# A decoder block on one Trainium2 core: v between the first two score steps, the last scores ahead of two gate projections, and the next block's k behind them

## What is computed

```python
h = rms_norm(x, ln_g)
proj = einsum('bsd,de->bse', h, w_in)
(u_pool, g_pool, c_a, c_b, g_conv, q, k, v, g_attn) = split_columns(proj)
y_pool = pool_mixer(u_pool, pool_w, pool_scale)
y_conv = conv_module(c_a, c_b, conv_dw, conv_b, conv_ln_g, conv_ln_b, conv_pw)
y_attn = sliding_window_attention(q, k, v, sinks)   # 8 heads, 2 kv heads, window 128, ALiBi, sinks
y = concat([y_pool * silu(g_pool), y_conv * silu(g_conv), y_attn * silu(g_attn)])
out = rms_norm(x + einsum('bse,ed->bsd', y, w_out), final_g)
```

## Time and profile before

| what | value |
|---|---|
| median of 3 runs | 1454.54 us (1451.94 to 1455.07) |
| the profiled execution's own time | 1452.87 us |
| its span in the profile | 1450.7 us, 20622 instructions |
| busy: PE, DVE, ACT, POOL | 94%, 81%, 38%, 35% |
| mean granted clock of PE | 0.986 |
| chain that ended last | PE 66%, DVE 14%, DMA 8%, ACT 5%, POOL 3% |

### The profile page before, as it was taken

The page is one execution under the profiler, slowest core; times in us unless marked ns, Lnnn a source line. Parts: engine busy times, 40 slices in busy tenths (PEclk is TensorE's granted clock), DMA queues, the critical chain, the costliest instruction groups (busy, mean ns, idle before and its releaser), DMA issues.

```text
span 1450.7 us, 20622 instructions
## 1 busy us (share of the span) xinstructions
PE 1363.4 (94%) x7070; PEld 1112.5 (77%) x7070; DVE 1170.9 (81%) x2365; ACT 549.3 (38%) x1421; POOL 504.8 (35%) x640
## 2 busy tenths in 40 slices
PE   6989898989989899876999999999999999999998
PEld 5867676767778687755888888888888888888886
DVE  4877768685868675554989999989899998888886
ACT  5746555555555554330221221121222243333332
POOL 5254545445354534552010010110101255555552
PEclk9999999999999999988999999999999999999999
DMA  9757482939384736657031230330326756545531
GB/s 214 218 125 263 124 284 89 288 110 268 124 254 153 203 146 162 245 130 222 12 131 54 108 131 24 136 130 14 131 88 250 286 193 213 164 158 163 159 126 73
DMA packets 112426, 230.78 MB, mean 159 GB/s; under 512 B 16464, under 2 KB 74192, under 8 KB 104656
## 3 DMA queue, kind: packets, MB, share of 16 engines
q1 hardware_dynamic: 88192, 205.85, 42.5%
q10 hardware_dynamic: 24144, 23.80, 6.8%
HBM read 131.05 MB, written 98.57 MB: 158 GB/s over the span
## 4 chain that ended last, share of the span: by engine, by line
PE 66%; DVE 14%; DMA 8%; ACT 5%; POOL 3%; issue 2%; SPq 1%; POOLq 0%; ACTq 0%; DVEq 0%
PE wide L346 12%; PE wide L347 12%; PE wide L348 12%; DMA xs<-in_x_dram 5%; PE pair L1239 3%; PE pair L1233 3%; PE pair L1234 3%; DVE m_tail L1994 3%; DVE a_rows L1038 2%; ACT a_rows L909 2%; PE wide L1233 2%; PE wide L1234 2%; PE turn L1202 2%; PE wide L1239 2%; PE turn L347 2%
## 5 line engine op out<-in xcount | busy, mean ns | idle before, releaser
L1994 DVE SCALAR_TENSOR_TENSOR m_tail<-m_tail,m_taps 128x512 f32<-128x512 f32 x480 | 338.5, 750 | 4.6
L1233 PE MATMUL pair<-xT,w_hi 128*128 128x512 f32 x384 | 154.5, 402 | 27.0 <-ACT xT L333 23.5
L845 POOL TENSOR_SCALAR a_rows<-a_rows,a_inv 128x128 f32<-128x128 f32 x256 | 108.4, 443 | 204.1 <-DVE a_inv L1058 204.0
L1736 POOL TENSOR_TENSOR operand_sums<-m_y 128x512 f32<-128x512 f32 x75 | 102.2, 1362 | 167.7 <-PE wide L348 116.6
L108 POOL TENSOR_TENSOR pool_carrier<-pool_carrier 128x1 f32<-128x1 f32 x23 | 14.0, 611 | 394.5 <-DVE m_meanvar L2003 394.5
L1234 PE MATMUL pair<-xT,w_lo 128*128 128x512 f32 x384 | 150.8, 393 | 0.0
L1239 PE MATMUL pair<-xT,w_hi 128*128 128x512 f32 x384 | 149.2, 394 | 0.9 <-DVE xT L339 0.7
L346 PE MATMUL wide<-x_first,w_hi 128*128 128x512 f32 x320 | 125.4, 392 | 0.0
L346 PE MATMUL wide<-xT,w_hi 128*128 128x512 f32 x320 | 125.2, 391 | 0.0
L348 PE MATMUL wide<-x_first,w_hi 128*128 128x512 f32 x320 | 124.6, 389 | 0.0
L348 PE MATMUL wide<-xT,w_hi 128*128 128x512 f32 x320 | 124.5, 389 | 0.0
(11 more groups left out here) (262 smaller groups left out, 3233.8 us busy)
## 6 DMA issues: line engine op xcount, KB each, us to landing
xT_scratch<-xT SPq DMA_DIRECT2D x16, 2048.0 KB, 10.3
p_scratch<-a_rows SPq DMA_DIRECT2D x32, 512.0 KB, 2.6
x_first<-xT_scratch SPq DMA_DIRECT2D x16, 1024.0 KB, 8.7
xT<-xT_scratch SPq DMA_DIRECT2D x16, 1024.0 KB, 9.0
combo_scratch<-stage SPq DMA_DIRECT2D x28, 512.0 KB, 5.3
m_y<-y_scratch ACTq DMA_DIRECT2D x14, 1024.0 KB, 6.6
xs<-in_x_dram SPq DMA_DIRECT2D x20, 512.0 KB, 10.7
a_pT<-p_scratch SPq DMA_DIRECT2D x64, 128.0 KB, 4.7
```

The costliest lines, as they stand in the source:

```text
L845: last = nc.gpsimd.tensor_scalar(probs[b][:, h], probs[b][:, h], inv[:, b, h:h + 1], 0.5, ALU.mult, ALU.mult)
L1233: nc.tensor.matmul(out, w.hi(c)[:, kk, cols], st.hi[:, kk, :], start=(kk == 0), stop=False)
L1736: nc.gpsimd.tensor_tensor(operand_sums[:, i, 1], y_block(q, left), y_block(q, right), SIGN[op]).then_inc(operand_sum, 1)
L1994: nc.vector.scalar_tensor_tensor(out=conv[:, i, :], in0=h[:, i, j:j + TB], scalar=taps[:, i, j:j + 1], in1=conv[:, i, :], op0=ALU.mult, op ...
```

## The change

It moves work in five queues and adds or removes none, apart from waits.

- **PE**: k of block n+1 now stands behind g3 of block n, at the end of the body. A block starts with attend(n-1, 0), then q0 to q3, the fold now in q3; then the wait for q_taken and scores 0; then attend(n-1, 1), v, scores 1, g0, scores 2 (with turn_v), g1, scores 3, g2, g3. q0 and q1 wait for one half of the last scores only.
- **ACT**: scales of the next x stand at the end: part 0 ahead of the exponentials of j = 0, parts 1 and 2 behind those of j = 3, part 3 behind the tanh of g2; then split_hi 0 to 3. The squares stand behind q_hi 1, the copy of v between the exponentials of j = 0 and 1.
- **DVE**: the transposes of the next x stand with their scales (`next_x`), all the inverts of a step behind both halves of take_scores, gate_make one step later, split_lo 0 to 3 behind next_x(3). In block 7 the split of CHUNK_GP stands behind the inverts of j = 3.
- **POOL**: mask(n, 0) behind normalise 1 and mask(n, 1) behind normalise 2; masks 2 and 3 of the block before now stand ahead of the root.
- **SP**: the load of the next x stands first in a block, then the load of the probabilities 2, the store of 3, the load of 3.

```diff
--- before.py
+++ after.py
@@ -739,10 +739,10 @@
             else:
+                st.load(sp, n + 1, (0, 1))
+                load_probs(sp, n - 1, 2)
                 store_probs(sp, n - 1, 3)
-                st.load(sp, n + 1, (0, 1))
-                for j in (2, 3):
-                    load_probs(sp, n - 1, j)
+                load_probs(sp, n - 1, 3)
...
@@ -761,14 +761,14 @@
-        store_probs(sp, NB - 2, 3)
         combos.wait_stored(sp)
...
         sp.wait_ge(st.lo_done, KT * NB)
         for c in (CHUNK_CB, CHUNK_CA, CHUNK_GP):
             w.load(sp, c, (0, 1))
-        for j in (2, 3):
-            load_probs(sp, NB - 2, j)
+        load_probs(sp, NB - 2, 2)
+        store_probs(sp, NB - 2, 3)
+        load_probs(sp, NB - 2, 3)
         sp.wait_ge(xT_stored[PIECES - 1], 16)
         load_xT(sp, x_first, x_first_loaded, xT_scratch, 0, (3,))
...
@@ -860,18 +860,14 @@
             else:
-                mask(n - 1, 1)
+                for j in (2, 3):
+                    mask(n - 1, j)
             if n < NB - 1:
                 st.root(pool, n + 1, carrier)
-            if n > 0:
-                for j in (2, 3):
-                    mask(n - 1, j)
             for j in range(SUB):
                 normalise(n, j)
-                if j == 2:
-                    mask(n, 0)
-                    if n == NB - 1:
-                        mask(n, 1)
+                if j in (1, 2):
+                    mask(n, j - 1)
...
@@ -946,63 +942,63 @@
...
-            elif not final:
+            q_hi(n, 1)
+            if not first and not final:
                 st.square(act, n + 1)
-            q_hi(n, 1)
...
             q_hi(n, 2)
-            if not first and not final:
-                st.scale(act, n + 1, 0)
...
                 w.split_hi(act, CHUNK_CB)
-            else:
-                st.scale(act, n + 1, 1)
             q_hi(n, 3)
-            if not first and not final:
-                st.scale(act, n + 1, 2)
-            for s in combos.of_block(n, (3,)):
+            for s in combos.of_block(n, (3, 4)):
...
-            if first:
-                for part in (0, 1):
-                    st.scale(act, 1, part)
-            act.wait_ge(st.squared, SUB + st.HALF * (n if final else n + 1))
-            copy_out(n, slot("v"), vT)
-            for s in combos.of_block(n, (4,)):
-                combos.split_hi(act, s)
-            if not first and not final:
...
+            def take_v():
+                act.wait_ge(st.squared, SUB + st.HALF * (n if final else n + 1))
+                copy_out(n, slot("v"), vT)
+
...
+            if not final:
+                st.scale(act, n + 1, 0)
+            for kv in range(KV):
+                exps(n, 0, kv)
+            take_v()
+            for kv in range(KV):
+                exps(n, 1, kv)
+            gate_tanh(n, 0)
+            exps(n, 2, 0)
+            spread_v()
+            exps(n, 2, 1)
+            gate_tanh(n, 1)
+            if final:
+                w.split_hi(act, CHUNK_GP)
+            for kv in range(KV):
+                exps(n, 3, kv)
+            if not final:
+                for part in (1, 2):
+                    st.scale(act, n + 1, part)
+            gate_tanh(n, 2)
+            if not final:
                 st.scale(act, n + 1, 3)
-            if first:
-                st.scale(act, 1, 2)
-            for j in range(SUB):
-                exps(n, j, 0)
-                if j == SUB - 1 and not final:
-                    for kk in range(st.AHEAD):
-                        st.split_hi(act, n + 1, kk)
-                if final and j == 2:
-                    w.split_hi(act, CHUNK_GP)
...
-                if j:
-                    gate_tanh(n, j)
-                exps(n, j, 1)
-                if j == 0:
-                    gate_tanh(n, j)
-                if first and j == 0:
...
+                for kk in range(st.AHEAD):
+                    st.split_hi(act, n + 1, kk)
+            gate_tanh(n, 3)
...
@@ -1108,69 +1104,67 @@
...
+            make_k_lo(n)
             if not first:
+                output(dve, n - 1, 0)
                 turn_squares_of_probs(SUB * n - 1)
-            make_k_lo(n)
             make_q_lo(n, 0)
             make_combos(n, (0,))
-            if not first:
-                output(dve, n - 1, 0)
-                if not final:
-                    st.square_more(dve, n + 1)
...
-                if t == 1 and not first and not final:
+                if t == 3 and not final:
                     st.mean(dve, n + 1)
                 make_q_lo(n, t)
-                if t == 3 and not first and not final:
-                    st.turn_squares(dve, n + 1, 1)
+                if t == 1 and not first and not final:
+                    st.square_more(dve, n + 1)
...
-                elif t == 2 and not final:
-                    st.turn_squares(dve, n + 1, 0)
-                elif t == 3 and first:
-                    for part in (0, 1):
-                        st.turn_squares(dve, 1, part)
-                elif t == 3 and not final:
-                    st.turn_squares(dve, n + 1, 2)
...
+            def next_x(part):
+                if not final:
+                    st.turn_squares(dve, n + 1, part)
+
+            take_scores(n, 0, 0)
+            take_scores(n, 0, 1)
             if not first:
                 output(dve, n - 1, 1)
-            for j in range(SUB):
+            inverts(0)
+            for j in range(1, SUB):
                 take_scores(n, j, 0)
-                if j in (1, 2):
-                    turn_squares_of_probs(SUB * n + j - 1)
+                turn_squares_of_probs(SUB * n + j - 1)
                 take_scores(n, j, 1)
-                invert(4 * n + j, j % 2, 0)
-                if j == 3:
-                    turn_squares_of_probs(SUB * n + 2)
-                if first and j < 2:
-                    st.turn_squares(dve, 1, 2 + j)
-                elif j == 0 and not first and not final:
-                    st.turn_squares(dve, n + 1, 3)
-                if j == SUB - 1 and not final:
-                    st.split_lo(dve, n + 1, 0)
-                if j:
-                    gate_make(n, j)
-                if j == SUB - 1 and not final:
-                    for kk in range(1, PIECE):
-                        st.split_lo(dve, n + 1, kk)
-                invert(4 * n + j, j % 2, 1)
-                if j == 0:
-                    gate_make(n, j)
-                if final and j == 2:
-                    w.split_lo(dve, CHUNK_GP)
+                if j == 1:
+                    next_x(0)
+                inverts(j)
+                if j < 3:
+                    gate_make(n, j - 1)
+            if final:
+                w.split_lo(dve, CHUNK_GP)
+            for part in (1, 2):
+                next_x(part)
+            gate_make(n, 2)
+            next_x(3)
+            if not final:
+                for kk in range(PIECE):
+                    st.split_lo(dve, n + 1, kk)
+            gate_make(n, 3)
...
         turn_squares_of_probs(SUB * NB - 1)
+        for name in ("g2", "g3"):
+            dve.wait_ge(free(slot(name)), earlier(NB - 1, slot(name)) + 1)
...
@@ -1220,7 +1214,7 @@
...
             if name[0] == "q":
-                need(pe, score_taken, 2 * SUB * n)
+                need(pe, score_taken, 2 * SUB * n - (1 if name in ("q0", "q1") and n > 0 else 0))
             else:
...
@@ -1283,36 +1277,39 @@
...
                 project(n, "k", lambda kk: st.transpose(pe, kk + TURNS) if kk + TURNS < KT else None)
-                project(n, "q0")
             else:
-                project(n, "k")
-                project(n, "q0")
                 attend(pe, n - 1, 0)
-            final = isinstance(n, int) and n == NB - 1
-            for name in ("q1", "q2", "q3", "v"):
-                project(n, name, folding(n) if name == ("q3" if first else "q2") and not final else None)
+            for name in ("q0", "q1", "q2", "q3"):
+                project(n, name, folding(n) if name == "q3" and not final else None)
             pe.wait_ge(q_taken, GROUP * (n + 1))
+            scores(n, 0)
...
-            for j in range(SUB):
-                scores(n, j, turn_v if j == 1 else None)
-                project(n, f"g{j}")
+            project(n, "v")
+            scores(n, 1)
+            project(n, "g0")
+            scores(n, 2, lambda: turn_v(n))
+            project(n, "g1")
+            scores(n, 3)
+            project(n, "g2")
+            project(n, "g3")
             if final:
                 attend(pe, n, 0)
+            else:
+                project(n + 1, "k")
```

31 lines of the change are left out of this document (16 added, 15 removed).

## The result

The changed kernel takes 1521.67 us (median of 4 runs, 1514.09 to 1522.44), the kernel before 1454.80 us in the same comparison: the ratio is 1.045, with a 95% interval of 1.0415 to 1.0488. It is slower, as forecast, but by 67 us where 36 us were forecast, and 1521.67 us lies outside the range of 1460 to 1504 us. The profiled execution took 1521.13 us.

A forecast was written before the change was run, and what follows sets the result against it. PE was taken to bound the attention phase, with DVE not far behind. The terms -20.1 - 3.4 + 19.4 + 6.4 + 34.7 + 1.6 - 11.3 + 8.9 gave +36.2 us on 1452.87 us: 1489 us, range 1460 to 1504 us.

The forecast's parts named there:

- part 1: The fold moves from q2 to q3, 5.57 us later; waits gone -13.7 us, clock losses gone -6.4 us: -20.1 us.
- 2, scores 3: The wait of 0.48 us at scores 3 goes in seven blocks, as DVE gets longer between steps: -3.4 us.
- part 3: Scores 0 directly behind q3 newly wait for q's copy, +19.4 us; clock loss behind those waits, +6.4 us.
- part 4: k behind g3 waits 7.9 us for x; the boundary costs 9.45 us instead of 4.5, seven times: +34.7 us.
- Part 5: Block 7: PE reaches the masks of attend(6, 1) earlier, +1.6 us; the loss at attend(7, 0) goes, -11.3 us.
- Part 6: Seam to the mixer phase: x_first's load starts later, delaying SP's queue and the last attend step: +8.9 us.
- the cover works: At k: x's chain finishes inside g2 and g3, so k starts without a wait; 1423 us, chance 0.07.

The follow-up runs named there:

- e1: The changed kernel with POOL's masks 2 and 3 put back behind the root; ratio to the kernel before 1.0689.
- e2: The changed kernel with all 16 squares of the next x on ACT and none on DVE; ratio to the kernel before 1.0305.
- e9: The kernel before with only the load of the next x put ahead of the store of probabilities 3 in SP's queue; ratio to the kernel before 0.9868.
- e4: The changed kernel with the scalings of the next x spread over the block on ACT; ratio to the kernel before 1.0131.
- e6: The changed kernel with e2, e4 and e5 together, and gate_make 2 ahead of the transposes of j = 3; ratio to the kernel before 1.0048.
- e3: The changed kernel with attend(n-1, 1) ahead of the wait for q_taken and of scores 0; ratio to the kernel before 1.0405.
- e7: e6 with the edit of e3 added; ratio to the kernel before 1.0061.
- e5: The changed kernel with the low-part split of CHUNK_GP put back ahead of DVE's last score step in block 7; ratio to the kernel before 1.0402.

## Why the prediction was wrong

Term by term, in us, forecast and measured (measured from the waits and durations of the profiled executions; the parts sum to 68, the spans differ by 68.5):

| part | forecast | measured | from |
|---|---|---|---|
| 1, fold | -20.1 | +16.0 | waits 21.9 - 13.7; 18 matmuls of q3 14.2 slower, less 6.4 before |
| 2, scores 3 | -3.4 | -2.8 | 1.0 - 3.8 |
| 3, scores 0 | +19.4 and +6.4 | +19.1 and +7.0 | waits; slow scores, attend and v behind four of eight |
| 4, k | +34.7 | +34.3 | waits 52.0, k's own 13.8 too long, less 7 x 4.5 |
| 5, block 7 | +1.6 and -11.3 | -6.1 and -11.3 | no wait left at either attend step; attend(6, 1) itself 1.1 shorter |
| 6, seam | +8.9 | +11.8 | 34.1 - 22.3 |

**The step that failed is part 1**, and in it one clause: "It moves one projection further, from q2 to q3, so 5.57 us later against the same squares". They were not the same squares: DVE's eight took 8 us instead of 3, and the fold waited 21.9 us where the sum had none. The change also moves POOL's masks 2 and 3 ahead of the root, and the stores and loads that feed them earlier. That puts them at 291.3 to 302.6 of that block, right where DVE squares from 296.0 on. I had seen, priced and even quoted the rule for this collision, in part 4, and looked for it only where the trace of before had an example. In part 1 I counted the removed wait and not what the moved engine would meet. e1 and e2 show the cause from two sides. The rest of the error is the clock behind it: each wait of 3.2 to 3.9 us was followed by half clock for a part of q3's rest (2.4 us lost on average), where four of the six waits of 1.7 to 2.7 us before had cost 1.6 us. The part's other half, the earlier x load, was right: e9 shows the fold's waits gone by that alone. Its 6.4 us for the clock were not to be had, since in e9 that loss moved to k.

**Part 5** erred the other way: I let PE arrive 1.6 us earlier at masks that stayed where they were, but masks 2 and 3 of block 6 were earlier too (-7.7 us against the forecast). The last of them ended 43.9 us behind k's start before and 37.0 us in the change, where scores 3 of block 6 stand one projection and the wait of k further ahead of that start; that this is what moved them is read from the order, and no run tried it. The shift hid a fifth of the error of part 1. **Part 6** was 3 us short, for an issue on SP of 6.2 us where I took 3.

**Parts 3 and 4 came out** within 1 us each, the forecast's whole argument for "slower". The paths were right; that the sums agree so closely is in part luck. In part 4 k waited 7.4 us and not 7.9, and lost 0.4 us more than forecast by itself (3 us each way over seven k's). In part 3 seven waits of 2.1 us instead of 2.3 made up for one of 4.3 us instead of 3.3, and the 6.4 us for the clock were the middle of a range from 0 to 12.8. e4 and e6 add what the prediction did not say: all of part 4 can be had back by moving scalings (46 us), while part 3 can't, since scores need spacing on either side (e3, e7). The rival "the cover works" was no way for this kernel to go, but its condition, scalings ahead of the last exponentials, is what e4 built, and it removed 42 of the 52 us of waiting.

Two things stay open. How much of k's 7.4 us is the masks' part wasn't tried by itself; in the rows of the changed kernel, three small operations of take_scores take 1.10, 0.82 and 1.33 us in that block, one of the inverts of j = 2 between them 1.27 us, and 0.15 to 0.17 us where no mask runs. That makes 3.9 us, an estimate from these rows of the most that the masks can have cost, against the 5 us that the forecast took for two masks. And why one load of constants takes 6.2 us of issue in the change, 3.8 us in e5 and 3.1 us before wasn't tried either.

## What to carry to other kernels

When an engine's work is moved, go through every other engine's queue at its new time, not only at the places where it collides already: a wait that is "covered by 5 us" was lost to an operation that grew from 0.42 to 1.34 us beside a moved neighbour. Look at the waits of the engine that is waited for as well: the kernel before had PE wait 13.7 us for ACT, and ACT 33.8 us for a load, and only the second tells what to move. A change of many moves can hold one that is worth having: the single exchange of two lines in SP's queue gave 1.3%, and was invisible inside a change that lost 4.5%. And the rest of a wait that is removed is found where the next one of the same chain stands: see which semaphore the engine waits for after each mend (xT, then a_gate; a_q, then a_rowmax).

## What the runs showed of the hardware

- The clock behind a wait depends on more than the wait. In the change six fold waits of 3.2 to 3.9 us were each followed by half clock (0.50) for 3.5 to 6 us of matmuls; k's waits of 6.5 to 7.8 us by k's own 7.0 to 8.0 us in place of 6.8; of the eight waits of 2.1 to 4.3 us ahead of scores 0, four by slow scores, and of two waits of 2.10 us in consecutive blocks one was and one was not. k's two waits of 1.6 to 1.7 us cost no clock in the kernel before, and with the fold's waits gone (e9) they were followed by slow matmuls at most k's: a mean clock does not rise by all that one wait had cost.
- An issue on SP's queue is not of one length: the two parts of the x load took 1.4 to 1.9 us to issue behind a store (before) and 0.85 us ahead of it (e9), and the same constants 3.1, 3.8 and 6.2 us in three kernels.
